# Sixteen conditional blocks of four engines, nested or one after another

## What is computed

```python
eid = (grp[:, None] * EXPERTS_PER_GROUP + i_top).reshape(-1)   # two experts per token
counts = jnp.bincount(eid, length=N_EXPERTS)
...
def expert_block(args):
    xb, e = args
    hb = jax.nn.silu(xb @ w_gate[e]) * (xb @ w_up[e])
    return hb @ w_down[e]
...
y = yb.reshape(-1, d)[dest] * gate.reshape(-1)[order][:, None]
return jnp.zeros_like(xt).at[tok].add(y).reshape(shp)
```

## Time and profile before

| | |
|---|---|
| median of three runs | 1795.76 us (1794.34 to 1795.99) |
| the profiled execution | 1795.99 us, of which its span 1794.2 us |
| PE busy | 1495.8 us (83%) |
| DVE, ACT, POOL busy | 577.9 us, 269.8 us, 70.9 us |
| read and written in HBM | 586.63 MB and 17.48 MB, 337 GB/s over the span |
| granted TensorE clock, mean | 0.904 of 2.4 GHz |

### The profile page before, as it was taken

How to read it: one execution, slowest core, us unless ns; L and a number is a source line. 1 busy time by engine, 2 the same in 40 slices (tenths; PEclk the granted TensorE clock), 3 DMA queues, 4 the chain that set the end, 5 groups by cost and what they waited for, 6 DMA issues and landing times.

```text
span 1794.2 us, 25175 instructions
## 1 busy us (share of the span) xinstructions
PE 1495.8 (83%) x10680; PEld 870.2 (49%) x10680; DVE 577.9 (32%) x1210; ACT 269.8 (15%) x618; POOL 70.9 (4%) x88
## 2 busy tenths in 40 slices
PE   3999999999698999948997867878769677888684
PEld 2787788888576577723333322323223223232231
DVE  0744476687454111163321211112102111121026
ACT  0012311201263100021111100110101011111110
POOL 2110000111110000000000000000000000000000
PEclk9999999999898899969998988889889888788895
DMA  9996387896899898319989999999999999999991
GB/s 279 315 294 202 103 264 239 254 315 196 312 365 379 290 293 313 138 37 418 418 331 419 419 419 419 419 419 419 419 419 418 419 419 420 419 420 419 419 387 53
DMA packets 236255, 597.41 MB, mean 333 GB/s; under 512 B 13984, under 2 KB 173280, under 8 KB 179808
## 3 DMA queue, kind: packets, MB, share of 16 engines
q1 hardware_dynamic: 216320, 499.22, 73.6%
q0 software_dynamic: 9792, 75.57, 10.8%
q10 hardware_dynamic: 10024, 20.94, 3.2%
HBM read 586.63 MB, written 17.48 MB: 337 GB/s over the span
## 4 chain that ended last, share of the span: by engine, by line
DMA 33%; PE 26%; SPq 2%; DVE 2%; ACT 1%; issue 1%; ACTq 0%; DVEq 0%
DMA arena<-in_w_up 32%; PE ps L1816 7%; PE ps L1871 6%; PE ps L1901 5%; PE ps L1845 4%; PE ps L1892 2%; SPq L1394 2%; DMA arena<-in_w_down 2%; PE ps L1852 0%; PE ps L1807 0%; ACT arena L1461 0%; DVE arena L1773 0%; DVE arena L1774 0%; SPq L1396 0%; PE ps L1805 0%
## 5 line engine op out<-in xcount | busy, mean ns | idle before, releaser
L1871 PE MATMUL ps<-arena 128*32 128x256 f32 x4352 | 318.8, 439 | 178.4 <-DMA arena<-in_w_up 176.9
L638 PE MATMUL ps<-arena 128*128 128x264 f32 x1664 | 382.9, 388 | 28.4 <-DMA arena<-in_w_in 28.4
L638 PEld LDWEIGHTS ps<-arena 128*128 128x128 f32 x1664 | 313.2, 191 | 82.1 <-issue 27.0
L1871 PEld LDWEIGHTS ps<-arena 128*32 128x32 f32 x4352 | 170.5, 122 | 326.5 <-issue 272.6
L1845 PE MATMUL ps<-arena 128*32 128x512 f32 (+1 forms) x816 | 188.1, 1030 | 10.7 <-DVE arena L1664 10.7
L1679 DVE TENSOR_TENSOR arena<-arena,ps 64x256 f32<-64x256 f32 x34 | 14.4, 425 | 546.6 <-ACT arena L1465 546.6
L1892 PE MATMUL ps<-arena 128*32 128x512 f32 x1088 | 160.6, 693 | 3.1 <-DMA arena<-in_w_down 3.1
L1816 PE MATMUL ps<-arena 128*128 128x264 f32 x512 | 122.0, 396 | 1.4 <-PEq L2007 1.4
L1478 ACT COPY arena<-ps 32x512 f32<-32x512 f32 x136 | 78.4, 576 | 254.1 <-PE ps L1892 252.9
L1901 PE MATMUL ps<-arena,keep 128*128 128x512 f32 (+3 forms) x216 | 113.3, 685 | 3.5 <-issue 3.5
L1816 PEld LDWEIGHTS ps<-arena 128*128 128x128 f32 x512 | 97.6, 194 | 24.1 <-issue 7.8
(11 more groups left out here) (404 smaller groups left out, 1012.0 us busy)
## 6 DMA issues: line engine op xcount, KB each, us to landing
arena<-in_w_gate SPq DMA_DIRECT2D x128, 1024.0 KB, 26.6
arena<-in_w_up SPq DMA_DIRECT2D x128, 1024.0 KB, 27.0
arena<-in_w_down SPq DMA_DIRECT2D x128, 1024.0 KB, 27.1
arena<-in_w_in SPq DMA_DIRECT2D x52, 1024.0 KB, 7.1
arena<-in_w_o SPq DMA_DIRECT2D x16, 1024.0 KB, 11.0
arena<-in_w_cmp_k POOLq DMA_DIRECT2D x8, 512.0 KB, 8.1
arena<-in_w_cmp_v POOLq DMA_DIRECT2D x8, 512.0 KB, 6.8
arena<-in_win_k SPq DMA_DIRECT2D x8, 512.0 KB, 7.1
```

The costliest lines, as they stand in the source:

```text
L638: last = pe.matmul(ps[:, n % 2, 0:T], ring[:, n % FRONT_SLOTS, k, :], x[:, k, :], start=(k == 0), stop=(k == KT - 1))
L1871: last = pe.matmul(ps[BS * q:BS * q + BS, 0, 0:CHUNK // 2], xs[:, kk * 4 + i, :], ring[:, s, at:at + CHUNK // 2], start=(k == 0), stop=(k ...
```

## The change

In the four engine functions, the recursive `over(i)`, which puts the condition of block i+1 inside the body of block i, becomes a loop over i with 16 conditions one after another. The bodies are the same. The diff, whole:

```diff
--- before.py
+++ after.py
@@ -1412,18 +1412,13 @@
                 sp.wait_ge(S["used"], n_wo + 12 * NE + k - NSLOT + 1)
                 sp.dma_start(ln2[k], a[name].broadcast_to([P, D])).then_inc(S["f_ln"], 16)
             n_over = extra(sp)
-
-            def over(i):
+            for i in range(NOVER):
                 with sp.If(n_over > i):
                     eid = sp.value_load(m.over[0:1, i:i + 1], min_val=0, max_val=NE - 1)
                     for j in range(12):
                         s, _, free = over_slot(12 * i + j)
                         sp.wait_ge(S["used"], free)
                         weights(s, eid, j)
-                    if i + 1 < NOVER:
-                        over(i + 1)
-
-            over(0)
             sp.wait_ge(S["f_st"], 48)
 
         @block.scalar
```

## The result

The change made the kernel slower: 1861.21 us median (1859.26 to 1865.76, four runs) against 1795.05 us, ratio 1.0376 with a 95% interval of 1.0352 to 1.0399, which is 63 to 72 us. The forecast was 1853 us, +57.1, with 1841 to 1862 as its own range.

The account below looks back on a forecast made before the run. PE's branch before the last 24 matmuls bounds the end; 11 jumps at 4.39 us plus 4 at 3.3, less the old 4.39, add 57.1 to 1796.0: 1853 us, own range 1841 to 1862, whole range 1813 to 1893.

Parts of the forecast that it names:

- What bounds: Near the end, PE's one 4390 ns branch outlasts ACT's copies by 1.09 us; delaying the units at 1752.08 delays the end.
- How far, and where they land: PE's further bodies: 443 instructions, 1.77 pages each; of 16 jumps one is free, 11 skip a page, 4 reach the next.
- The price: PE's jumps: 4.39 us for each page skipped, 3.3 us into the next page; +57.1 us after subtracting the old jump.
- A2: PE's skipping jump waits for the page between to land first, 7.7 us each: +93.5 us, 1889.5; chance 0.22.
- B: PE holds several pages ahead; first jumps find targets, then the stream limits: +19 us, 1815, or +62 at 3.3 each; chance 0.12.
- C: Short PE jumps stay within loaded code, 50 to 190 ns each: not slower, saves at most 1.0 us, 1795.0; chance 0.06.
- D: PE's 4390 ns is its queue draining, paid once; DVE then bounds: 0 to +10 us, about 1800; chance 0.05.
- The other engines: Code waits at their branches, DVE 14 to 25 us, ACT some 4, SP 10 to 15, all hidden behind PE.

Follow-up runs that it names:

- The first two experiments: Against the kernel before: conditions one after another on PE alone, 1858.37 us, ratio 1.0366; then on SP, ACT and DVE with PE nested, 1794.19 us, ratio 1.0008.

## Why the prediction was right, point by point

**What bounds.** Right. With weights and ACT's copies out of the way, PE's jump was what the end waited for, and the new jumps lengthened that wait: 65.1 us more of it, and from the start of the 24 matmuls to the end it is 42.1 us, as before. The first two experiments put the loss on PE.

**How far, and where they land.** Right in its counts: 443 instructions or 1.77 pages by body gave one free jump, eleven that skip a page and four that do not, and the trace has them so, with 25 more packets where some 26 were forecast. (The 20 additional packets that the same text names elsewhere are a slip.) Which jumps are the cheap ones says more: it is the 1st, 5th, 9th, 12th and 16th. If each cheap jump lands one page on and each other one two pages on, that order fits only a body of 1.71 to 1.75 pages; with 443 instructions this is, by my estimate, 253 to 258 to a page, so the 250 was a little low and the 1.77 a little high. That the counts came out is in part luck: with 1.77 pages and the branch 50 instructions into its page, the 15 jumps cover 27 pages and not the 26 of the text, 12 skips and three others, and the sixth jump is cheap and not the fifth.

**The price.** A jump into the next page was put at 3.3 us and is 3.0 to 3.6. The first one was to take below 0.2 us and takes 0.38. The skipping jump was put at 4.39 us and is 4.95: this is the term that was mis-sized. 11 x 0.56 = 6.2 us, with 0.4 us for the four others, and 0.4 for the first and 0.9 for the gaps between records, which the sum left out, brings 57.1 to 65.0 us, and the chain has 65.1. The 4.39 us was the price of one packet while data still moved (DMA share 0.32), which started 1.8 us after the comparison; with quiet queues it starts after 1.0 to 1.5 us, and one packet costs 3.3 to 3.8 us, as the loads between the jumps and the jumps behind the units (3612 and 3768 ns) show. In the change the queues are quiet from the second skip on, but two pages are fetched at once. I had both directions in my range and took a value between them for the wrong reason: the fall and the rise partly cancel, and that the forecast came within 9 us is in part luck.

**Rivals.** A2, a skip that first waits for the page between, would be 7.7 us each; no record is above 5.7, and pairs of packets run side by side. The page between is paid for, but in shared transfer, not by waiting in line. B (several pages held ahead) and C (not slower) needed short records for the 2nd to 4th jump; the first of the three starts at 1744.2 and is the longest of all. (B's +62 us at 3.3 us a page leaves out the last latency of 3.3 us that its +19 has.) D (a draining queue, paid once) is out by fifteen records of 3.0 us and more, and by an 89 ns branch at the same place when PE falls through. The two-page window of the Trainium skill, "Runtime: NRT & Kernel Launch", section "Instruction fetch mechanics", agrees with one free jump, eleven and four; eight blocks held ahead, the reading behind B and C, do not, and the measurement decides.

**The other engines.** Hidden, as said. DVE took 11 us for its sixteen, against 14 to 25 forecast; SP 15.7 us, just over its 10 to 15; ACT 2.6 us, against one crossing of some 4 us. Their longest record is 76 ns, so DVE's sixteen fill 0.9 of its 11 us. Most of the rest is three gaps between its records (four or five crossings were forecast), of 4.3, 2.0 and 1.9 us; here are the two records around each of the first two:

```profile
L1735 DVEq COMPARE_BRANCH  x2: 56/56/56, 1737.5 to 1741.8; - x2
L1735 DVEq COMPARE_BRANCH  x2: 56/56/56, 1742.4 to 1744.4; - x2
```

At least one packet of q14 starts in each of the three. I read them as waits for code, which show on this engine as a gap behind the branch and on PE inside its record. No run separates them from another cause.

## What to carry to other kernels

In these runs a condition that fails costs PE 0.2 to 0.5 us if its target is in the page of code at hand or the loaded one behind it, and 2.7 to 5.7 us if not, whether it passes one body or sixteen. So rare code is nested, or put behind one condition, so that the usual case passes all of it in one jump, and that jump goes where PE would wait anyway. Code that never runs can cost time, and the number of instruction packets in the profile is a sign of it: q8 has 112 with PE's conditions one after another, 93 in groups of four, 96 with short bodies, and 87 in each kernel where PE passes all further blocks in one jump.

## What was not expected of the hardware

Of two packets of instructions under way together the durations added up to 3.5 and 4.0 us, of one alone to 0.88 to 1.35 (the last ahead of the 3768 ns record), and in the pair of 3.5 us no other queue moved anything. Whether they shared one DMA engine, or the engine's memory was the limit, no run here tells.
